# A decoder trunk's first loads split and reordered, and its query tiles drained in a row

## What is computed

```python
for l in range(DEPTH):
    u = rms_norm(x, norm1_w[l])
    proj = u @ w_in[l]
    (cx, cb, cc, gq, gk, gv, gr, ga, sq, sk, sv, gates) = jnp.split(proj, split_idx, axis=-1)
    ya = short_conv_mixer(cx, cb, cc, conv_w[l], conv_b[l])
    yb = gla_mixer(gq, gk, gv, gr, ga, gla_wa2[l], gla_ba[l], gla_onorm_w[l])
    yc = swa_mixer(sq, sk, sv, positions, q_norm_w[l], k_norm_w[l], sinks[l])
    ...
    x = x + mixed @ w_o[l]
    h = rms_norm(x, norm2_w[l])
    x = x + jnp.square(jax.nn.relu(h @ w_up[l])) @ w_down[l]
```

## Time and profile before

| | |
|---|---|
| median of 3 runs | 1614.15 us (1614.03 to 1615.59) |
| the profiled execution | 1614.83 us, span 1613.0 us |
| mean granted clock of TensorE | 0.996 |
| busy: PE, weight loads, DVE, ACT | 1586.1, 1302.6, 1011.3, 723.2 us (98%, 81%, 63%, 45%) |
| the chain that ended last | PE 97%; ACT, SP's queue and DVE 1% each |
| first DMA issues, of SP and of ACT | at 0.73 us |
| first product of a projection | at 20.48 us |
| moved by DMA | 151.11 MB, 94 GB/s |

### The profile page before, as it was taken

The page is one execution under the profiler, slowest core; times in us unless marked ns, Lnnn a source line. Parts: engine busy times, 40 slices in busy tenths (PEclk is TensorE's granted clock), DMA queues, the critical chain, the costliest instruction groups (busy, mean ns, idle before and its releaser), DMA issues.

```text
span 1613.0 us, 21047 instructions
## 1 busy us (share of the span) xinstructions
PE 1586.1 (98%) x7536; PEld 1302.6 (81%) x7536; DVE 1011.3 (63%) x1428; ACT 723.2 (45%) x1106; POOL 0.2 (0%) x4
## 2 busy tenths in 40 slices
PE   5999999999999999999999999999999999999999
PEld 4877778888888888888887877788888888888887
DVE  3576775445646969696346667745554578686952
ACT  4446563222336455544335475523233373636350
POOL 0000000000000000000000000000000000000000
PEclk9999999999999999999999999999999999999999
DMA  4331123223352141415022212223333514141301
GB/s 148 105 105 53 57 75 105 79 78 105 105 209 79 52 157 52 157 40 174 1 73 85 79 53 79 79 79 103 106 104 105 183 53 153 57 150 60 139 18 52
DMA packets 107574, 151.11 MB, mean 94 GB/s; under 512 B 4912, under 2 KB 81232, under 8 KB 107472
## 3 DMA queue, kind: packets, MB, share of 16 engines
q1 hardware_dynamic: 107040, 149.69, 27.9%
q10 hardware_dynamic: 432, 0.08, 0.0%
HBM read 147.67 MB, written 2.10 MB: 93 GB/s over the span
## 4 chain that ended last, share of the span: by engine, by line
PE 97%; ACT 1%; SPq 1%; DVE 1%; DMA 0%; DVEq 0%; ACTq 0%; issue 0%
PE acc L519 19%; PE acc L520 19%; PE acc L521 19%; PE acc L541 7%; PE acc L543 7%; PE acc L542 7%; PE acc L572 5%; PE acc L571 5%; PE acc L570 5%; PE bank L708 1%; PE bank L727 1%; PE bank L587 1%; PE bank L719 1%; PE bank L666 1%; PE bank L680 0%; DMA raw<-in_w_in_dram 0%
## 5 line engine op out<-in xcount | busy, mean ns | idle before, releaser
L519 PE MATMUL acc<-uh,wh 128*128 128x512 f32 x1152 | 453.3, 393 | 7.1 <-DVEq L1032 7.0
L521 PE MATMUL acc<-uh,wl 128*128 128x512 f32 x1152 | 449.1, 390 | 0.0
L520 PE MATMUL acc<-ul,wh 128*128 128x512 f32 x1152 | 449.0, 390 | 0.0
L519 PEld LDWEIGHTS acc<-uh,wh 128*128 128x128 f32 x1152 | 216.6, 188 | 58.0 <-DVE wl L1015 7.4
L804 ACT ACTIVATE wh<-raw 128x1024 fp32r<-128x1024 f32 x144 | 152.5, 1060 | 238.9 <-PE acc L521 147.3
L521 PEld LDWEIGHTS acc<-uh,wl 128*128 128x128 f32 x1152 | 216.5, 188 | 45.6
L520 PEld LDWEIGHTS acc<-ul,wh 128*128 128x128 f32 x1152 | 216.8, 188 | 43.8
L1015 DVE TENSOR_TENSOR wl<-raw,wh 128x1024 fp32r<-128x1024 f32 x144 | 176.4, 1225 | 89.3 <-ACT wh L804 77.9
L804 ACT ACTIVATE wh_rows<-raw_down 128x1024 fp32r<-128x1024 f32 x100 | 106.2, 1062 | 133.9 <-PE acc L572 35.5
L1015 DVE TENSOR_TENSOR wl_rows<-raw_down,wh_rows 128x1024 fp32r<-128x1024 f32 x100 | 122.5, 1225 | 58.6 <-ACT wh_rows L804 51.3
L1041 DVE TENSOR_TENSOR gate_tanh<-acc,rsqrt_rows 128x512 f32<-128x512 f32 x48 | 33.2, 691 | 116.2 <-PE acc L521 116.0
(11 more groups left out here) (223 smaller groups left out, 2452.9 us busy)
## 6 DMA issues: line engine op xcount, KB each, us to landing
raw<-in_w_in_dram SPq DMA_DIRECT2D x40, 1024.0 KB, 5.2
raw<-in_w_up_dram SPq DMA_DIRECT2D x32, 1024.0 KB, 5.9
raw_down<-in_w_down_dram SPq DMA_DIRECT2D x32, 1024.0 KB, 8.2
raw_branch<-in_w_in_dram SPq DMA_DIRECT2D x12, 1024.0 KB, 5.0
raw_branch<-in_w_branch_dram SPq DMA_DIRECT2D x12, 1024.0 KB, 5.0
raw_branch<-in_w_o_dram SPq DMA_DIRECT2D x8, 1024.0 KB, 5.1
x_tokens<-in_x_dram SPq DMA_DIRECT2D x4, 512.0 KB, 5.6
raw_kv<-in_w_in_dram SPq DMA_DIRECT2D x4, 512.0 KB, 3.7
```

The lines of the kernel that those rows point to most:

```text
L519: nc.tensor.matmul(a[:], wh[slot][:, k, :], right_h, start=at_k == 0, stop=False)
L520: nc.tensor.matmul(a[:], wh[slot][:, k, :], right_l, start=False, stop=False)
L521: last = nc.tensor.matmul(a[:], wl[slot][:, k, :], right_h, start=False, stop=at_k == n - 1)
```

## The change

Five things change.

- x comes in halves of columns. The right halves are loaded first, tiles 0 and 1 on SP's queue, 2 and 3 on ACT's, where they stand ahead of the positions. Then SP loads the lower rows of the first slab (k = 4 to 7) into the slot's second half, the left halves of x, the slab's other rows, and gk0's slab ahead of the parameter loads. The masks come after these.
- gq0 and gq1 are split by halves of k, with semaphores of their own: gq0's upper half, then UT4 to UT7, then gq1's upper half, both lower halves, gk0.
- TensorE transposes the identity 16 times into a bank as soon as the constants are there, and then waits for x's right halves; UT0 waits for the left halves.
- ACT's order puts each `ss` behind a `UT` in place of two ahead of it, and the zeroing of a mask buffer (`attz`) later; DVE takes `RN` after UT3 in place of after UT0; TensorE takes `NROW` after gq1.1.
- The four query tiles are taken in a row: ACT's `ZB` comes after sq3 in place of after sq0, DVE's split of gv2 and `X0` after sq3 in place of between the tiles, and TensorE has `KT0` and `KT1` two and one token tiles' work later. DVE's waits for the masks move from ahead of the layers to `ZB` and `ATT0` of the first.

```diff
--- before.py
+++ after.py
@@ -29,6 +29,8 @@
 QUARTERS = 4
 SPLIT = 4
 AHEAD = 3
+FIRST = ("gq0", "gq1")
+WARM = 16
 TOKEN_KINDS = ("kva", "sq", "gv", "gr", "wa", "wb", "db", "da")
 PRODUCTS = 7
 PRODUCT = (0, 4, 5, 2, 3, 1, 6)
@@ -58,22 +60,22 @@
     return unit, [int(c) for c in some] if some else list(whole)
 
 
-PE_ORDER = """gq0.0 gq1.0 UT0 gk0.0 UT1 gk1.0 UT2 UT3 NROW gq0.1 gq1.1 gk0.1 gk1.1 kva0 kva1 kva2 kva3 sq0.012 AT sq0.3 sq1.0 ZA
-sq1.123 sq2 sq3 gv0.01 KT0 gv0.23 gv1 gv2 gv3.01 KT1 gv3.2 ATT0 KD gv3.3 QT0 gr0.0 ATT1 QT1 gr0.1 QT2 gr0.2 SC0 QT3
-gr0.3 gr1.01 SC1 KV0 gr1.23 PT0 gr2.01 KV1 PV0 gr2.23 gr3.0 PT1 SC2 gr3.12 SC3 gr3.3 GO0 cx0.0 GO1 PV1 cx0.1 cx1.0 PT2
-cx1.1 cx2.0 PV2 cx2.1 cx3 cc0.0 PT3 SC4 cc0.1 PV3 SC5 YT0 cc1 cc2 cc3.0 YT1 PT4 cc3.1 SC6 YT2 PV4 cb0 PT5 YT3 cb1.0
-SC7 PV5 cb1.1 cb2 PT6 cb3 PV6 gate0.0 PT7 gate0.1 gate1.0 PV7 gate1.1 gate2 gate3""".split()
-
-
-ACT_ORDER = """+gk1 attz ss0 ss1 UT0 ss2 ss3 UT1 UT2 UT3 +kva0 +kva1 +kva2 +kva3 +sq0 +sq1 +sq2 kva0 kva1 kva2 kva3 +sq3 +gv0 ZA +gv1
-+gv2 sq0 ZB sq1 sq2 +gv3 sq3 KT0 +gr0 +gr1 +gr2 gv0 gv1 KT1 gv2 KD +gr3 gv3 QT0 QT1 QT2 QT3 +cx0 SC0 SM0 SC1 +cx1 PT0
+PE_ORDER = """gq0.0 gq1.0 UT0 gk0.0 UT1 gk1.0 UT2 UT3 gq0.1 gq1.1 NROW gk0.1 gk1.1 kva0 kva1 kva2 kva3 sq0.012 AT sq0.3 sq1.0 ZA
+sq1.123 sq2 sq3 gv0 gv1.01 KT0 gv1.23 gv2 gv3.012 KT1 ATT0 KD gv3.3 QT0 gr0.0 ATT1 QT1 gr0.1 QT2 gr0.2 SC0 QT3 gr0.3
+gr1.01 SC1 KV0 gr1.23 PT0 gr2.01 KV1 PV0 gr2.23 gr3.0 PT1 SC2 gr3.12 SC3 gr3.3 GO0 cx0.0 GO1 PV1 cx0.1 cx1.0 PT2 cx1.1
+cx2.0 PV2 cx2.1 cx3 cc0.0 PT3 SC4 cc0.1 PV3 SC5 YT0 cc1 cc2 cc3.0 YT1 PT4 cc3.1 SC6 YT2 PV4 cb0 PT5 YT3 cb1.0 SC7 PV5
+cb1.1 cb2 PT6 cb3 PV6 gate0.0 PT7 gate0.1 gate1.0 PV7 gate1.1 gate2 gate3""".split()
+
+
+ACT_ORDER = """+gk1 UT0 ss0 UT1 ss1 UT2 ss2 UT3 ss3 +kva0 +kva1 attz +kva2 +kva3 +sq0 +sq1 +sq2 kva0 kva1 kva2 kva3 +sq3 +gv0 ZA +gv1
++gv2 sq0 sq1 sq2 sq3 ZB +gv3 KT0 +gr0 +gr1 +gr2 gv0 gv1 KT1 gv2 KD +gr3 gv3 QT0 QT1 QT2 QT3 +cx0 SC0 SM0 SC1 +cx1 PT0
 SM1 PV0 +cx2 gr0 PT1 gr1 gr2 SC2 gr3 +cx3 GO0 SC3 SM2 GO1 +cc0 SM3 PV1 PT2 mz1 +cc1 mz2 mz0 mz3 PV2 +cc2 +cc3 PT3 SC4
 +cb0 YT0 PV3 SM4 +cb1 SC5 +cb2 SM5 YT1 PT4 +cb3 YT2 PV4 SC6 +gate0 PT5 YT3 SM6 cb0 PV5 +gate1 SC7 +gate2 PT6 SM7 cb1
 cb2 +gate3 PV6 PT7 +br0 cb3 gate0 PV7 +br1 gate1 +br2 gate2 gate3""".split()
 
 
-DVE_ORDER = """+gk1 UT0 RN UT1 UT2 UT3 +kva0 NROW gk0 +kva1 +kva2 gk1 +kva3 +sq0 +sq1 +sq2 kva0 kva1 kva2 kva3 +sq3 AT +gv0 ZA ZB
-+gv1 sq0 +gv2 X0 sq1 sq2 sq3 +gv3 QS +gr0 QM +gr1 X1 QR +gr2 ATT0 +gr3 ATT1 SC0 +cx0 SM0 SC1 KV0 SM1 +cx1 KV1 PV0 +cx2
+DVE_ORDER = """+gk1 UT0 UT1 UT2 UT3 RN +kva0 NROW gk0 +kva1 +kva2 gk1 +kva3 +sq0 +sq1 +sq2 kva0 kva1 kva2 kva3 +sq3 AT +gv0 ZA ZB
++gv1 sq0 sq1 sq2 sq3 +gv2 X0 +gv3 QS +gr0 QM +gr1 X1 QR +gr2 ATT0 +gr3 ATT1 SC0 +cx0 SM0 SC1 KV0 SM1 +cx1 KV1 PV0 +cx2
 gr0 SC2 gr1 gr2 SC3 gr3 +cx3 SM2 GO0 SM3 cx0 GO1 OS YG0 cx1 YG1 +cc0 +cc1 cx2 +cc2 PV1 PV2 cx3 +cc3 SC4 cc0 ct0 SM4
 SC5 +cb0 YT0 +cb1 cc1 PV3 SM5 cc2 +cb2 YT1 cc3 SC6 +cb3 YT2 PV4 SM6 cv0 +gate0 YT3 ct1 SC7 cl0 ct2 SM7 PV5 cv1 cv2
 +gate1 +gate2 cl1 ct3 +gate3 PV6 cv3 cl2 +br0 cl3 gate0 PV7 gate1 +br1 gate2 +br2 gate3""".split()
@@ -322,6 +324,7 @@
         in_full, masks_full, pos_full, gm_full, nw_full, par_full, out_full = map(
             sem, "in_full masks_full pos_full gm_full nw_full par_full out_full".split())
         x_full = [sem(f"x_full{i}") for i in range(TT)]
+        x_right = [sem(f"x_right{i}") for i in range(TT)]
         raw_full = [sem(f"raw_full{i}") for i in range(2)]
         raw_free = [sem(f"raw_free{i}") for i in range(2)]
         down_full = [sem(f"down_full{i}") for i in range(PAIRS)]
@@ -334,14 +337,14 @@
...
-         diff_ready, b12_summed, b11_summed, b21_summed, b22_summed, angle_ready, sines_ready) = map(sem, """
+         diff_ready, b12_summed, b11_summed, b21_summed, b22_summed, angle_ready, sines_ready, first_full, first_hi, first_lo) = map(sem, """
...
-         diff_ready b12_summed b11_summed b21_summed b22_summed angle_ready sines_ready""".split())
+         diff_ready b12_summed b11_summed b21_summed b22_summed angle_ready sines_ready first_full first_hi first_lo""".split())
 
         UNIT_CREDIT = SPLIT
 
@@ -426,11 +429,6 @@
         @block.sync
         def _(sp):
             sp.dma_start(cst[:, 0:CC["scan"]], consts[:, 0:CC["scan"]]).then_inc(in_full, 16)
-            for t in range(TT):
-                sp.dma_start(x_tok[:, t, :], x[0, t * P:(t + 1) * P, :]).then_inc(x_full[t], 16)
-
-            sp.dma_start(cst[:, CC["scan"]:], consts[:, CC["scan"]:]).then_inc(masks_full, 16)
-
             def load(l, u, source, into=None):
                 slot = SLAB[u] % 2
                 sp.wait_ge(raw_free[slot], slab_count(l, u))
@@ -450,13 +448,27 @@
                 else:
                     load(l, u, rows(w_in, l, 0, KT, COL[kind] + i * P, SLAB_COLS))
 
+            def x_half(half):
+                cols = slice(half * SEQ, (half + 1) * SEQ)
+                for t in range(TT - 2 * half):
+                    sp.dma_start(x_tok[:, t, cols], x[0, t * P:(t + 1) * P, cols]).then_inc((x_full, x_right)[half][t], 16)
+
+            x_half(1)
+            sp.wait_ge(raw_free[0], 1)
+            sp.dma_start(raw[0][:, KT // 2:, :], rows(w_in, 0, KT // 2 * P, KT // 2, COL["gq"], SLAB_COLS)).then_inc(first_full, 16)
+            x_half(0)
+            sp.dma_start(raw[0][:, 0:KT // 2, :], rows(w_in, 0, 0, KT // 2, COL["gq"], SLAB_COLS)).then_inc(raw_full[0], 16)
             for l in range(DEPTH):
-                project(l, "gq0")
+                if l:
+                    project(l, "gq0")
+                project(l, "gk0")
                 sp.wait_ge(par_free, l + 1)
                 sp.dma_start(raw_ga[:], rows(w_in, l, 0, KT, COL["ga"], GLA_RANK)).then_inc(par_full, 16)
                 sp.dma_start(par[:], params[l]).then_inc(par_full, 16)
                 sp.dma_start(wa2[:], gla_wa2[l]).then_inc(par_full, 16)
-                for u in PROJ[2::2]:
+                if l == 0:
+                    sp.dma_start(cst[:, CC["scan"]:], consts[:, CC["scan"]:]).then_inc(masks_full, 16)
+                for u in PROJ[4::2]:
                     project(l, u)
                 for g in range(N_BRANCH):
                     for half in range(2):
@@ -507,8 +519,13 @@
                 n, slot, a = k_tiles(u), unit_at(l, u) % SPLIT, acc[ACC_BANKS[u][0]]
                 order = [(k + n // 2) % n if back else k for k in range(n)]
                 if 0 in pieces:
+                    if l == 0 and u in FIRST:
+                        pe.wait_ge(first_lo, FIRST.index(u) + 1)
+                    else:
+                        pe.wait_ge(lo_done, unit_at(l, u) + 1)
+                    open_acc(l, u)
+                elif l == 0 and u in FIRST:
                     pe.wait_ge(lo_done, unit_at(l, u) + 1)
-                    open_acc(l, u)
                 if gate is not None:
                     gate()
                 for at_k in range(n // 2 * pieces[0], n // 2 * (pieces[-1] + 1)):
@@ -596,8 +613,10 @@
                 last.then_inc(bank_full, 1)
 
             pe.wait_ge(in_full, 16)
+            for _ in range(WARM):
+                nc.tensor.transpose(bank[3][:, 0:P], ident, ident)
             for t in range(TT):
-                pe.wait_ge(x_full[t], 16)
+                pe.wait_ge(x_right[t], 16)
             for k in range(KT // 2, KT):
                 transposed_x(0, f"UT{k}", in_full, 16)
 
@@ -615,6 +634,8 @@
                         if l:
                             transposed_x(l, word, x_upd, 16 * l)
                         else:
+                            for t in range(TT):
+                                pe.wait_ge(x_full[t], 16)
                             transposed_x(l, word, in_full, 16)
                     elif kind == "NROW":
                         rows(l, word, rs_ready, rst)
@@ -772,6 +793,8 @@
 
         @block.scalar
         def _(act):
+            for t in (2, 3):
+                act.dma_start(x_tok[:, t, SEQ:], x[0, t * P:(t + 1) * P, SEQ:]).then_inc(x_right[t], 16)
             act.dma_start(pos_i[:], positions).then_inc(pos_full, 16)
             act.dma_start(nw[:], norms).then_inc(nw_full, 16)
             act.dma_start(gm[:], gmask).then_inc(gm_full, 16)
@@ -825,10 +848,15 @@
             nc.scalar.activation(sin8[:], angle[:, 0], ACT.Sin)
             nc.scalar.activation(angle[:, 2], angle[:, 0], ACT.Sin, scale=0.5).then_inc(sines_ready, 1)
             act.wait_ge(nw_full, 16)
-            for pos in range(AHEAD):
-                split_high(0, PROJ[pos])
+            act.wait_ge(first_full, 16)
+            nc.scalar.activation(split_view(True, "gq0")[:, KT // 2:], raw_view("gq0")[:, KT // 2:], ACT.Copy).then_inc(first_hi, 1)
             for k in range(KT // 2, KT):
                 norm_high(0, f"UT{k}", 0)
+            nc.scalar.activation(split_view(True, "gq1")[:, KT // 2:], raw_view("gq1")[:, KT // 2:], ACT.Copy).then_inc(first_hi, 1)
+            act.wait_ge(raw_full[0], 16)
```

(26 more changed lines are left out.)

## The result

The changed kernel takes 1602.38 us, the median of six runs (1601.81 to 1603.29), against 1614.51 for the kernel before beside it: 12.1 us less, a ratio of 0.9924 with a 95% interval of 0.9911 to 0.9937. The profiled run took 1602.7 us, with a span of 1600.9 where it was 1613.0, and a mean granted clock of 0.999. The forecast was 1601.4.

What follows compares the result with a forecast made beforehand. TensorE, busy 98% of the span, bounds the kernel, so only its waits and low-clock time can be won. Front 7.7, normalising tiles -2.2, query tiles 7.2 make 12.7 us: span 1602.1, median 1601.4, range 1597 to 1607.

Steps and rivals of the forecast that it cites:

- The front: Start of the kernel: the positions' chain, not the data, sets the first product at 12.8, 7.7 us earlier.
- Half a slab in at about 8: Front: half the first weight slab lands about 8 us, some 5.5 at the same 2 MB.
- The cover behind it: After the first product: DVE's lows to gk0 end about 19.3, TensorE arrives 20.3, covered by 1 us.
- The transposes of the identity: Front: sixteen warming transposes are off the path and bring no gain; first products again at the low clock.
- The normalising tiles: UT0 to UT3, ss, NROW: new waits make each layer 1.1 us worse, 2.2 in all.
- the 0.5 lost before: gq0.1 in the kernel before: four tiles of k took 3.3 us where 2.7 are needed.
- The query tiles: Query tiles in a row: 5.0 us regained, 1.4 lost, so 3.6 us in a layer, 7.2 in both.
- The sum: Whole kernel: 7.7 - 2.2 + 7.2 = 12.7 us faster, a median of 1601.4; within 2.5 us, chance 0.55.
- The first: Rival: gq0.1 and KD run without a pause; 17.2 us faster, 1597; chance 0.18.
- The second: Rival: positions land at 9.0 and KD's pause brings the low clock; 6.9 us faster, 1607.2; chance 0.20.
- The third: Rival: query tiles in a row don't help, DVE's reads still hold TensorE; 2.9 us, 1611.3; chance 0.04.
- The fourth: Rival, slower: positions starved behind x and weights; whole gain gone if they land at 19.3; chance 0.03.

Runs made afterwards that it cites:

- the two runs on these orders: Query-tile orders put back in the changed kernel: 1610.26 us; only the query tiles taken in a row, on the kernel before: 1607.83 us.
- the fastest kernel: The changed kernel with the positions issued first on ACT's queue and KD behind gv3.3: 1599.21 us, 0.9906 of the kernel before.

## Why the prediction was right, step by step

**The front.** Right in mechanism. The angles' chain, not the data, set the start; putting the positions first took 2.8 us off the first product of this profile, 2.1 off that of the other runs. The chain from the landing on was summed right: second sine ended at 11.29, 3.8 after the landing at some 7.45, gq0's upper low at 12.6, first product 0.93 after the first normalised low (12.53 to 13.46). The term that was off is the landing: 7.45 where I took 6.6, inside its bounds of 5.5 to 9.0. That is 0.7 of the 7.7 in this profile; in the runs with the landing at 5.0 to 5.2 after issue the first product came at 12.63 to 12.87, within 0.2 of the 12.8. "Half a slab in at about 8" is borne out by the split at 8.39 once the positions no longer hid it. The cover behind it held: no wait between the first product and gq0.1, 7.15 us to UT0 where it had been 7.01.

**The transposes of the identity.** Right: nothing for the path, and the low clock at the first product. Leaving them out changed nothing that can be told from no change (1602.11 against 1602.38).

**The normalising tiles.** 1.1 us a layer forecast, 1.32 and 1.21 measured against the kernel before. gq0.1 took 4.38 us (27.81 to 32.19) where it took 3.28: 1.10 more, almost all of it the wait of 1.13. I had a wait of 1.4 and counted the 0.5 lost before as replaced by it; the wait was shorter and those 0.5 stayed. The rest is mostly NROW's, which takes 0.5 of TensorE's time where it took 0.35. What the forecast did not see is that this is no price of the order ss2 ahead of UT3 alone: the wait is one of several that fall due close together. Row sums, roots, NROW, the banks of gq and gk, the splits of kva and the slabs they free form one chain, and each edit gave the wait to the next link (gq0.1, NROW, gk1's bank, kva0's bank behind the slab of sq2) with no gain in the total. That it is one chain is read from the traces of these runs; no edit shortened a link of it to see the total follow.

**The query tiles.** Closest. With the 5.56 us gained up to kva0 taken off, the forecast's times and the measured ones are: ACT's fourth square 78.3 and 78.44, ZB's table load 79.0 and 79.10, X0's start 83.6 and 83.57, the rotation's end 101.8 and 101.65. KT0 ran at 86.06 and KT1 at 99.02 with no wait (0.3 at KT1 with these orders on the old front). TensorE came to KD at 100.74 where 100.4 was summed, so it waited 1.09 rather than 1.35. The gain was 3.64 in layer 1 and 4.05 in layer 2 against 3.6. The 0.4 lies in ACT's third square: in layer 1 it starts at 77.06, 36.05 us behind kva0, after a wait of 1.15 for DVE's first sum, which is late; in layer 2 at 868.86, 35.65 behind kva0, as soon as TensorE has its tile. The sum used layer 1's times, with that wait in them, for both layers. The exchange of one wait for the other is shown both ways by the two runs on these orders.

**The sum.** 7.7 - 2.2 + 7.2 = 12.7 against 7.0 - 2.5 + 7.7 = 12.2. Three small errors, of both signs: 0.7 too much at the front, 0.3 too little for the normalising tiles' cost, 0.5 too little for the query tiles. These are of the profile. The median, 1602.38, is 1.0 above the forecast of 1601.4; 0.4 of that is the median of before, 1614.51 beside the changed kernel and 1614.15 in the forecast. That the three errors cancel in part is luck; each is small by itself.

**The rivals.** The first (no new waits) fell: both new waits are in the profile. The second came in one half and small: the positions were late by 0.8, not 2.4, and the 1.1 us waits never tipped the clock. The third fell with line 1170's wait gone. The fourth was right in its mechanism, that a later landing is a later first product, and far from its point.

## What to carry to other kernels

Follow the smallest load of a front to its last user: 2 KB of positions behind 0.5 MB of x on one queue set the start, and the order of two lines was worth 2 us. Where a wait is one of several that fall due within a microsecond, an order that removes it hands it on; price the links behind it in the profile before counting the gain, and expect two good edits to add up only if they are on different chains. Moving a block of work on one engine past another could here be summed to 0.3 us at the last consumer, and closer on the way, from the profile's own durations, as every instruction behind it was taken along. Sum each layer by itself, though: a wait in one of them made 0.4 us.

## What the runs showed of the hardware

- Small loads were late by what was issued around them, not by their size. The positions, 2 KB, landed 2.1 us after issue when first in ACT's queue, 2.1 to 2.2 when first with x's halves behind, and 5.0 to 5.8 with two halves ahead. What starts the other queue mattered as well: the 68.5 KB of constants, first on SP's queue in every kernel, took 3.3 to 4.2 us with x first on ACT's queue and 1.9 to 2.0 with the positions first there. The Trainium skill, "DMA: Bandwidth & Descriptors", section on queues, rings and completion order, says that a DMA's signal lands only after every earlier write of that DMA engine, across its queues. The rows agree with it, but none tells that from plain sharing of the engines.
- Sixteen transposes at the start took 3.65 us (0.228 each), and x's sixteen behind them 2.70 (3.64 with none ahead, 1.94 at the least). No clock record lies there; that the clock rose meanwhile is read from these durations.
- A granted clock of 1.00 over a stretch can be wrong where records are few: 13 to 17 us without the transposes, above. The spacing of the products tells it there.
- The length of a pause alone does not tell whether the clock falls. Before the first product TensorE idled 1.86 us in the fastest kernel and the clock stayed; it idled 1.85 with the query orders put back, and the clock fell 0.9 us into the products. x's sixteen transposes ahead of the pause had taken 1.94 us in the former and 3.10 in the latter. Stretches of 13 to 17 us, the latter kernel first:

```profile
13.00:17.00 4.00, 4.00 (x11) 2.91 (x11) 3.45 (x6) 3.02 (x5) 0.00 (x0) 0.58 1.05 281
```

```profile
13.00:17.00 4.00, 4.00 (x18) 2.82 (x17) 2.26 (x4) 1.90 (x3) 0.00 (x0) 1.00 1.14 304
```

  In these runs TensorE's pauses of 1.4 us or less were followed by no fall, those of 2.1 to 3.2 between transposes or products by one each time, by the spacing of the products; of those between, 1.78 (twice) and 1.86 had none, 1.85 and 1.90 had one. What decides is open. How long the low clock stayed differed too: 3.4 us in the changed kernel's front, some 6 with the normalising orders put back.
